# Two residual blocks on one Trainium2 core: in the last attention the turned gate is copied out of its bank by ScalarE, not VectorE

## The reference, cut to what matters

```python
q, k, v, gate = jnp.split(h @ w_in, ...)
q = rms_norm_2(q, q_norm_g); k = rms_norm_2(k, k_norm_g)     # per head, then axial rotary
pr = softmax(q @ k.T * scale)
o = pr @ v
return (o * silu(gate)) @ w_out
```

## Time and profile before

| | |
|---|---|
| median of 3 runs | 1054.5 us (1053.75 to 1055.5) |
| profiled execution: time | 1052.61 us |
| profiled execution: span | 1050.8 us |
| share of the span busy: PE, DVE, ACT | 93%, 69%, 52% |
| stretch with the changed items | 958 to 996 us |
| the copy (line 2363) | 8 instructions, 418 ns each |

### The profile page before, as it was taken

One profiled execution on the slowest core, in us unless ns is written; L12 is line 12 of the kernel. 1 busy time (PEld: TensorE's weight loads), 2 busy tenths in 40 slices (PEclk: granted clock), 3 DMA queues, 4 the chain that ended last, 5 costly groups with the idle time before them and its releaser, 6 DMA issues.

```text
span 1050.8 us, 14669 instructions
## 1 busy us (share of the span) xinstructions
PE 978.2 (93%) x5692; PEld 792.5 (75%) x5692; DVE 720.1 (69%) x1113; ACT 543.6 (52%) x869; POOL 49.2 (5%) x39
## 2 busy tenths in 40 slices
PE   6886998999999989999899999989999999998995
PEld 2663666989898866777699989877788887875684
DVE  3488668777776587565885554478654778797775
ACT  3367725544453253555355455435565746656662
POOL 0000003200000000000071100000000000000000
PEclk9999999999999989999999999999999999999998
DMA  9747476879897468332689776554434346551041
GB/s 350 245 145 295 161 240 214 287 258 341 298 328 261 160 238 294 127 118 64 200 269 254 209 234 188 183 190 132 149 121 130 121 141 200 187 174 61 32 160 40
DMA packets 106931, 204.85 MB, mean 195 GB/s; under 512 B 3488, under 2 KB 37680, under 8 KB 106864
## 3 DMA queue, kind: packets, MB, share of 16 engines
q1 hardware_dynamic: 103808, 193.25, 54.8%
q0 software_dynamic: 3056, 10.67, 3.5%
HBM read 202.76 MB, written 1.15 MB: 194 GB/s over the span
## 4 chain that ended last, share of the span: by engine, by line
PE 66%; DVE 17%; ACT 7%; DMA 6%; issue 3%; SPq 1%; ACTq 0%; DVEq 0%
PE bank L1672 13%; PE bank L1674 13%; PE bank L1673 13%; DVE w_lo L1851 5%; PE bank L1726 5%; PE bank L1728 4%; PE bank L1727 4%; DMA raw<-in_mlp_w 3%; PE bank L1747 2%; ACT w_hi L1293 2%; PE bank L1769 2%; DMA raw<-in_ada_w 2%; DMA raw<-in_ab_w_in 1%; PE bank L1574 1%; PE bank L1814 1%
## 5 line engine op out<-in xcount | busy, mean ns | idle before, releaser
L1851 DVE TENSOR_TENSOR w_lo<-raw,w_hi 128x2048 fp32r<-128x2048 f32 (+2 forms) x134 | 308.6, 2311 | 154.5 <-ACT w_hi L1293 153.4
L1293 ACT ACTIVATE w_hi<-raw 128x2048 fp32r<-128x2048 f32 (+2 forms) x134 | 248.5, 1857 | 131.3 <-PE bank L1674 69.2
L1672 PE MATMUL bank<-w_lo,ht_hi 128*128 128x512 f32 (+1 forms) x544 | 218.4, 401 | 12.5 <-DVE w_lo L1851 7.8
L1674 PE MATMUL bank<-w_hi,ht_lo 128*128 128x512 f32 (+1 forms) x528 | 206.4, 391 | 0.0
L1673 PE MATMUL bank<-w_hi,ht_hi 128*128 128x512 f32 (+1 forms) x528 | 206.1, 390 | 0.0
L1672 PEld LDWEIGHTS bank<-w_lo,ht_hi 128*128 128x128 f32 x544 | 103.7, 191 | 41.8 <-issue 21.4
L1726 PE MATMUL bank<-ht_hi,w_lo 128*128 128x256 f32 x448 | 127.5, 285 | 2.4 <-DVE w_lo L1851 2.4
L1727 PE MATMUL bank<-ht_lo,w_hi 128*128 128x256 f32 x448 | 126.8, 283 | 0.0
L1728 PE MATMUL bank<-ht_hi,w_hi 128*128 128x256 f32 x448 | 126.8, 283 | 0.0
L1674 PEld LDWEIGHTS bank<-w_hi,ht_lo 128*128 128x128 f32 x528 | 100.5, 190 | 21.3
L1673 PEld LDWEIGHTS bank<-w_hi,ht_hi 128*128 128x128 f32 x528 | 101.0, 191 | 18.8
(11 more groups left out here) (244 smaller groups left out, 1334.2 us busy)
## 6 DMA issues: line engine op xcount, KB each, us to landing
raw<-in_mlp_w SPq DMA_DIRECT2D x64, 1024.0 KB, 6.0
raw<-in_ada_w SPq DMA_DIRECT2D x44, 1024.0 KB, 5.3
raw<-in_a_w_in SPq DMA_DIRECT2D x16, 1024.0 KB, 5.3
raw<-in_c_w_in SPq DMA_DIRECT2D x12, 1024.0 KB, 5.4
raw<-in_b_w_in SPq DMA_DIRECT2D x10, 1024.0 KB, 5.1
raw<-in_ple_w_gate SPq DMA_DIRECT2D x8, 1024.0 KB, 5.0
raw<-in_ab_w_in SPq DMA_DIRECT2D x4, 1024.0 KB, 9.8
tok<-in_ada_w SPq DMA_DIRECT2D x4, 1024.0 KB, 12.8
```

The source lines that it names most:

```text
L1293: nc.scalar.activation(split_parts(n)[0], raw_tile(t), ACT.Copy).then_inc(high_done, 1)
L1672: nc.tensor.matmul(dst, a_hi[:, c, rows], lo[:, k, :], start=it["first"] and k == 0, stop=False)
L1674: mm = nc.tensor.matmul(dst, a_lo[:, c, rows], hi[:, k, :], start=False, stop=it["last"] and k == it["kc"] - 1)
L1851: nc.vector.tensor_tensor(lo, raw_tile(split[n]), hi.bitcast(F32), ALU.subtract).then_inc(low_done, 1)
```

## The change

`values(p)` now carries `prior`, the count at which bank 6 was freed by values(p-1). ScalarE gets a part in `values(p)` of this mode: it waits for the turned gate, and for `prior` (so that VectorE has read the last gate from `tmp_b`), copies bank 7 to `tmp_b` and frees bank 7. VectorE loses its wait for the turned gate and its copy; it waits for bank 7's count, which ScalarE now raises, and then multiplies as before.

```diff
@@ make_plan, attention
         def values(p, after=()):
-            return add("values", mode=held[p]["mode"], heads=held[p]["heads"], g=g0 + p, p=p, gate=gate_bank(p), banks=banks((6,)), after=evicted(*after),
+            prior = evicted(last_values[0]) if p else []
+            last_values[0] = add("values", mode=held[p]["mode"], heads=held[p]["heads"], g=g0 + p, p=p, gate=gate_bank(p), banks=banks((6,)), after=evicted(*after), prior=prior,
                        turned=evicted(next(i for i in plan if i["kind"] == "probs" and i["g"] == g0 + p)))
+            return last_values[0]
@@ block.scalar
+                elif kind == "values" and it["mode"] in GATED_OUT:
+                    turned_in, n = it["gate"][0]
+                    act.wait_ge(gates_turned, it["p"] + 1)
+                    if it["prior"]:
+                        for s, before in it["prior"]:
+                            act.wait_ge(bank_free[s], before)
+                    nc.scalar.activation(tmp_b[:, 0:S], bank[turned_in][:, 0:S], ACT.Copy).then_inc(bank_free[turned_in], 1)
@@ block.vector
                     b, used = it["banks"][0]
-                    dve.wait_ge(gates_turned, it["p"] + 1)
                     gate, (turned_in, n) = tmp_b[:, 0:S], it["gate"][0]
-                    nc.vector.tensor_copy(gate, bank[turned_in][:, 0:S]).then_inc(bank_free[turned_in], 1)
                     dve.wait_ge(bank_free[turned_in], n + 1)
```

More of the change, by code:

```diff
@@ L295, in attention @@
         held = {}
+        last_values = [None]
         def scores(p, turned, pairs=(2, 3), late=False):
```

## The result

| | before | changed |
|---|---|---|
| median, over 20 runs each | 1053.0 us | 1058.5 us |
| ratio to before | | 1.0047 (95% interval 1.0026 to 1.0068) |
| span of the profiled execution | 1050.8 us | 1057.8 us |

The changed kernel is 0.47% slower, 4.9 us of the median before by the ratio; the interval is 2.7 to 7.2 us. The forecast was 4.5 us (+0.43%), 1059.0, in a range of 1056.8 to 1061.6. The 1059.0 was counted from the 1054.5 us of three executions, and over 20 the kernel before takes 1053.0; so the absolute time comes within 0.5 us partly because this lower start and a somewhat larger difference (5.4 us between the medians) offset each other.

The account below looks back on a forecast made before the run. Dependences, with VectorE handing to an idle ScalarE, were taken to bound the stretch where four pairs run. Engine terms of 4.13 us plus 0.4 for the clock made 4.5, on 1054.5: 1059.0 us, range 1056.8 to 1061.6.

Parts of the forecast that it names:

- The loop: Pairs 0 to 3: minimum, four exponentials, copy, product, gate scaling, next minimum in series, adding 1.48, 1.47, 0.68, 0.23 us.
- the clock's share: At `turn_two(6)` and scores(4): TensorE's clock may fall after 3.5 us idle, adding 0 to 1.0 us, taken as 0.4.
- The price of the copy: ScalarE's copy of each gate: 0.39 us from start to release, bounds 0.27 and 0.56, and 0.27 in its queue.
- Pair 4's thin cover: At pair 4, waits for TensorE and ScalarE's split part cover the copy: 0 us added, 0.5 as upper bound.
- Pair 5's queue term: Pair 5's copy stands in ScalarE's queue ahead of `w_hi`, for which VectorE and TensorE waited: 0.27 us added.
- 1.48 and 1.47 us for the first two: Pairs 0 and 1: product delayed by 1.48 us, then 1.47 more, 2.95 in all, VectorE having had no pause before.
- Slack: Rival: VectorE's later pauses absorb the delay, only the first 1.48 us reaches the end, 1056.0 us; chance 10%.
- VectorE was relieved: Rival: ScalarE reaches the copy before VectorE's second minimum, gaining 0.45 us per pair, at most 3.6: 1050.9 us; chance 4%.
- The clock's further fall into the products with `b_w_out`: Rival: clock falls again or stays low into the first 12 such products, 2.6 us more, 1062.2 us; chance 10%.

Follow-up runs that it names:

- the clock kept up: Changed kernel plus 24 extra transposes of the identity on TensorE ahead of `turn_two(6)`: stretch 37.03 us, ratio to before 1.0051.
- VectorE held back: Kernel before, VectorE's own copy for pairs 0 to 5 waiting until ScalarE's exponentials of scores(p+2) freed their banks: ratio 1.0053; profiled again, stretch 38.15 us.

## Why the prediction was right

By its steps, measured from the first minimum of scores(2):

| | before | predicted | changed | changed again |
|---|---|---|---|---|
| product of pair 0 | 2.04 | 3.52 | 3.52 | 3.51 |
| minimum of scores(3) | 7.22 | 8.70 | 8.68 | 8.67 |
| product of pair 1 | 9.27 | 12.22 | 12.20 | 12.19 |
| minimum of scores(4) | 11.73 | 14.68 | 14.98 | 14.82 |
| product of pair 2 | 13.78 | 18.20 | 18.51 | 18.34 |
| minimum of scores(5) | 15.58 | 19.21 | 19.52 | 19.35 |
| product of pair 3 | 17.63 | 22.73 | 23.04 | 22.87 |
| minimum of scores(7) | 26.34 | 30.20 | 30.53 | 30.36 |
| `w_lo` behind pair 5 | 32.36 | 36.49 | 36.83 | 36.65 |

- **The loop.** The predicted column has the engines' terms alone, 4.13 us. It is right within 0.02 us up to pair 1. From scores(4) on, the changed kernel is 0.30 to 0.34 us later, which is the clock's share (I took 0.4); the kernel with the clock kept up measured it as 0.32. In the second execution it is 0.14 to 0.16. That the loop is closed by the copy's place is shown from both sides: with ScalarE's copy ahead of the exponentials the loss is gone, and with VectorE's own copy behind them it is there.
- **The size of the clock's term was partly luck.** I took 0.4 of 0 to 1.0 "since small transposes do not double". The transposes of `turn_two(6)` ran before the fall and kept their 0.66 us; what grew was scores(4), from 1.14 to 2.08, of which the cover ahead of VectorE took up the most. Where the fall came earlier (every copy twice, VectorE held back) they took 1.12 us and VectorE's wait was 0.46 longer.
- **The price of the copy.** 0.39 us, and 0.26 in the queue, where I took 0.27. Doubling it cost 0.28 us at each of five places.
- **Pair 4's thin cover** held: VectorE waited 0.20 us for TensorE at scores(7). With every copy twice that wait was gone.
- **Pair 5's queue term** was 0.27 us with only pairs 4 to 7 changed.
- **One thing was read too simply.** I gave each pair a term, 1.48 and 1.47 us for the first two, as if each were that pair's own. The sum is right only because the loop stays closed to pair 3. With pairs 0 and 1 alone, and no fall of the clock on the loop, 2.94 us arrive at scores(4), but only 2.25 at the end.
- **What the time alone can't say.** The interval of the ratio, 2.7 to 7.2 us, holds the forecast and much else; that the mechanism was right rests on the stretch and the experiments.
- **The rivals.** Slack did not take it up in the full change, though it takes 0.7 us of it when only the first two pairs change. VectorE was relieved only where the copy came first. The clock's further fall into the products with `b_w_out` was not seen in the two profiled executions of the changed kernel.

What stays open is what decides behind which idle time the clock falls.

## What to carry to other kernels

Moving an instruction between engines moves it to a place in another list, and the place can cost more than the instruction: here 0.39 us of copy became a wait of 1.84 us on the engine that was to be relieved. Before such a move, write down what stands ahead of it in the new list, what waits behind the old reader, and whether these two form a circle; if so, add up once round it. If the move is wanted anyway, put the instruction where the new engine is waiting, and read the effect in a stretch that starts behind the noise.

## What the hardware showed unexpectedly

- The same list of instructions ahead of the stretch took between 949.87 and 959.20 us in the profiles shown, 9 us apart, while the stretch of the kernel before repeated at 32.36 us in two executions. The difference goes with TensorE's granted clock: in the first of these two profiles it was 0.97 from 350 to 400 us, in the second 0.86. Of the executions of the kernel before that stand beside the experiments, the four fastest (1046.1 to 1046.7 us) had a mean of 0.986 to 0.988, and those over 1055 us one of 0.975 to 0.979. That one causes the other was not tested.
- The granted clock fell to 1.2 GHz behind idle times of TensorE of 3.52 and 3.53 us in the two executions of the changed kernel, of 3.81 with every copy twice, of 4.37 with VectorE held back, of 3.53 in the second execution with pairs 0 and 1, and of 1.97 in the kernel with extra transposes. It fell behind 1.49 us in the second execution of the kernel before, and behind 1.48 in the first it stayed. Behind 1.86 us in the changed kernel it stayed too, and behind 1.87 with pairs 0 and 1 it fell in one execution and stayed in the other. In the first execution with pairs 0 and 1 it did not fall behind 3.00 us; it had fallen 5 us before this idle time began and had come back.
- VectorE's wait for an exponential with an accumulator lasted until the accumulator had been read (960.50 us in the profile with VectorE held back), some 0.12 us after ScalarE had started its next instruction.
